# Hymba-style hybrid layer on one core: where the first phase's buffers lie, and where three chunks of W_out are loaded

## The chip, the cores and the metric

One Trainium2 chip (trn2), one of its cores. The metric is the device time of one launch in microseconds; the kernel before took 1374.45 us in the median of 3 runs.

## What is computed

One decoder layer: an input projection, two mixers side by side (windowed attention with sinks, and a Griffin recurrent branch), a gate and a norm for each, an output projection, a residual and a final norm. Everything is float32. Cut to what the change bears on:

```python
h = rmsnorm(x, ln_gain)                                    # x is (1, 2048, 1024)
z = einsum('bsd,de->bse', h, w_in)                         # q | k | v | gate A | recurrent input | gate B
y_attn = swa_sink_attention(q, k, v, sinks)                # window 128, 16 q heads, 4 kv heads of 64
y_attn = rmsnorm(y_attn * silu(g_attn), attn_out_gain)
y_lru = rg_lru(causal_depthwise_conv(x_lru), ...)
y_lru = rmsnorm(y_lru * silu(g_lru), lru_out_gain)
y = einsum('bse,ed->bsd', concatenate([y_attn, y_lru]), w_out)   # 2048 mixed channels to 1024
out = rmsnorm(x + y, final_gain)
```

## The kernel before, in words

Each product in float32 is made of three matmuls: every operand is split into a high part (a copy rounded by ScalarE, type fp32r) and a low part (operand minus high part, made by VectorE, in a few places by GpSimd), and high x high, high x low and low x high are summed in PSUM.

**First phase** (`phase_a`): 16 iterations, four quarters of 512 tokens by four groups of heads and channels. Each iteration projects nine weight groups (24 matmuls of 128x512 each, L1548), runs the attention of four 128-token blocks (`score`, `turn_p`, `weigh_v`), the recurrent gates and the scan, and stores its gated results (`hs0`, `hs1`, `ya`) to a DRAM scratch `y_scratch`, by DMAs that GpSimd issues in `write_out` (L702, L706). The signals `ya_out` and `yl_out` say that these stores have landed. In the last quarter TensorE no longer projects the next group's weights at the end, so the second phase is worked in there.

**Second phase** (`phase_b`): 16 token blocks of 128, two (s = 0, 1) in each of 8 steps. For a block, the 2048 mixed channels are 16 chunks of 128, and a chunk is 6 matmuls of 128x512 (three parts by two halves of the output). Chunks 0 to 7 are the attention's, chunks 8 to 15 the recurrent branch's; their sums stay apart, since each has its own norm, which VectorE multiplies in later (`add_group`).

**W_out** is loaded in 16 chunks of 128x1024 (`OutProjection.load_w`, on SP's DMA queue, L149) into the 3 slots of `w_raw`, chunk e into slot e % 3, each load after `low_w(e - 3)` has freed the slot. ScalarE then makes the high part (`high_w`, L164) and VectorE the low part (`low_w`, L169). Chunks 0 to 7 end in `split` (the first phase's h, free by then), chunks 8 to 15 in `wo_rest`, 64 KB a partition, which lies over the first phase's own buffers.

**The seam.** SP, ScalarE, VectorE, TensorE and GpSimd each run their part of both phases in the order in which it is written, without a barrier. At the start of the second phase ScalarE runs: the squares of block 0's y, `high_w(7)`, the high part of half of block 1's y, then it waits until the first phase is over and its stores have landed, says so (`b.over`), and goes on with `high_w(8)`. VectorE runs `low_w(7)`, `low_w(8)`, and then `mean_y(0, 0)`, the mean square of block 0's y, which it reads from the PSUM bank where TensorE summed it (`sum_squares`, L1998) and which TensorE needs back for chunk 8:

```python
act.wait_ge(*a.ya_done.at(NITER, 0))
act.wait_ge(*a.ya_out.at(NITER, 0))
for u in range(UNITS):
    act.wait_ge(*a.yl_out[u].at(NITER, 0))
act.sem_inc(b.over, 1)
proj.high_w(act, 8)
```

TensorE runs `begin(e)` (chunk e of block 0) and `second(e)` (chunk e of block 1) in the order begin(7), sum_squares(0, 0), begin(8), second(7), begin(9), sum_squares(0, 1), begin(10), begin(11), and then second(8), begin(12), second(9), begin(13), second(10), begin(14), second(11), begin(15), second(12) to second(15). After that comes step(1, 0), which reads `y_own` and waits for `low_y(1, 0)`. SP loads, in this order, chunks 7 to 10, then (after `b.over`) 11, x of block 0 into `res`, chunk 12, y of step 1 (`load_y(1, 0)`), chunks 13 to 15, x of block 1, the final gain (`fgain`), y of block 1 of step 1.

Of the kernel before, what the change touches and what calls it, by code (L numbers as in the profile page):

```python
# [23 lines left out]
F32R = mybir.dt.float32r  # L24
# [6 lines left out]
P = 128  # L31
# [94 lines left out]
ACC = {(0, 0): (0, 1), (1, 0): (2, 3), (0, 1): (0, 1), (1, 1): (2, 3)}  # L126


class OutProjection:


    def __init__(self, nc, both, b, w_out, y_dram):
        self.nc, self.both, self.b, self.w_out, self.y_dram = nc, both, b, w_out, y_dram
        blocks = lambda ap: ap.rearrange("p s d -> p (s d)").rearrange("p (e t) -> p e t", e=EC)
        self.y_raw = [blocks(both.rows[:, :, :]), blocks(both.rope[:, :, :])]
        self.y_hi = [both.y_own[:, 0, :, :], blocks(both.w_hi[:, 0:2, :])]
        self.y_lo = [both.y_own[:, 1, :, :], blocks(both.w_lo[:, 0:2, :])]
        self.first = both.split[:, :, :, :].rearrange("p q w (c d) -> p q w c d", c=4)
        self.rest = None

    def wo(self, e, low):
        if e >= EC // 2:
            return self.rest[:, e - EC // 2, low, :]
        return self.first[:, e // 4, low, e % 4, :]

    def load_w(self, sp, e):
        if e >= WSLOTS:
            sp.wait_ge(*self.b.wo_low.at(e - WSLOTS, 1))
        sp.dma_start(self.both.w_raw[:, e % WSLOTS, :], self.w_out[0, e * P:(e + 1) * P, :]  # L149
                     ).then_inc(*self.b.wo_in[e % WSLOTS].one())  # L150

    def load_y(self, sp, m, s):
# [8 lines left out]
    def high_w(self, act, e):  # L161
        s = e % WSLOTS
        act.wait_ge(*self.b.wo_in[s].at(e // WSLOTS, 1))
        self.nc.scalar.activation(self.wo(e, 0), self.both.w_raw[:, s, :], ACT.Copy,  # L164
                                  scale=self.both.egain[:, e:e + 1]).then_inc(*self.b.wo_high.one())

    def low_w(self, dve, e):
        dve.wait_ge(*self.b.wo_high.at(e, 1))
        self.nc.vector.scalar_tensor_tensor(  # L169
            out=self.wo(e, 1), in0=self.both.w_raw[:, e % WSLOTS, :], scalar=self.both.egain[:, e:e + 1],  # L170
            in1=self.wo(e, 0).bitcast(F32), op0=ALU.mult, op1=ALU.subtract).then_inc(*self.b.wo_low.one())

    def high_y(self, act, m, s):
# [100 lines left out]
def phase_a(nc, top, block, both, signals_b, proj, x, ln_gain, w_tiles, sinks, w_gates,  # L274
# [9 lines left out]
    with ExitStack() as ctx:  # L284
        signals = []

        def sb(name, shape, dt=F32):
            return ctx.enter_context(nc.sbuf_tensor(name, shape, dt))
# [10 lines left out]
        xs = sb("x_stat", [P, 4])
        table_sink = sb("table_sink", [P, 1])  # L300
        cosT, sinT, kraw, swp = (both.rope[:, i, :] for i in range(4))
        prev_mask = sb("prev_mask", [P, GQ, BLK], U8)
        cap = sb("cap", [P, 2, BLK])
        sink_all = sb("sink_all", [P, KV * GQ])
        sink_pairs = sink_all[:, :].rearrange("p (j s) -> p j s", s=2)
        prm = sb("prm", [P, NPRM, LRU_W // P])
# [4 lines left out]
        kc_ol = sb("kc_ol", [P, KV, BLK])
        k_carry, o_low = kc_ol[0:HD], kc_ol[HD:]
        vraw = sb("vraw", [P, 1 + NBLK, HD])
        v_hl = sb("v_hl", [P, 1 + NBLK, 2 * HD], F32R)
        dvraw = sb("dvraw", [P, NBLK, HD])
        dv_hl = sb("dv_hl", [P, NBLK, 2 * HD], F32R)
        v_carry = sb("v_carry", [P, KV, HD])
        qraw = sb("qraw", [P, T])
        qrot = sb("qrot", [P, T])
        q_hi = sb("q_hi", [P, 2, T], F32R)  # L320
        q_lo = sb("q_lo", [P, 2, T], F32R)

        s_sb = sb("s_sb", [P, 2, GQ, BLK + 1])
        p_sb = sb("p_sb", [P, 2, GQ, BLK + 1])
        smax = sb("smax", [P, 2, 4, GQ])
        sden = sb("sden", [P, 2, 2, GQ])
        p_hi = sb("p_hi", [P, GQ, BLK], F32R)
        p_lo = sb("p_lo", [P, GQ, BLK], F32R)
        p_hi_c = sb("p_hi_c", [P, GQ, BLK], F32R)
        p_lo_c = sb("p_lo_c", [P, GQ, BLK], F32R)  # L330
        o_sb = sb("o_sb", [P, 2, BLK])
        ya = sb("ya", [P, 2, T])
        xl = sb("xl", [P, CONV - 1 + T])
        cu = [sb(f"cu{u}", [P, T]) for u in range(UNITS)]
        u_hi = sb("u_hi", [P, T], F32R)
        u_lo = sb("u_lo", [P, T], F32R)
# [3 lines left out]
        ra = [sb(f"ra{u}", [P, T]) for u in range(UNITS)]  # L340
        a2 = sb("a2", [P, T])
        ri_all = sb("ri", [P, UNITS, T])
        ri = [ri_all[:, u, :] for u in range(UNITS)]
        gl = sb("gl", [P, T])
        hs = [sb(f"hs{u}", [P, T]) for u in range(UNITS)]
# [1361 lines left out]
        done.o_sum = o_sum  # L1707
        done.ya_out = ya_out
        done.yl_out = yl_out
        done.zeroed = zeroed  # L1710
        return done


def signals_of_phase_b(nc, top):
    b = Record()
    b.all = []

    def signal(name, per, unit=1):
# [24 lines left out]
    b.mean = signal("mean", 2)
    b.rooted = signal("rooted", 2)
    b.recip = signal("recip", 2)
    b.normed = signal("normed", 2)
    b.res_free = [signal(f"res_free{s}", 1) for s in range(2)]

    b.stored = [Signal(top, nc, f"stored{s}", 1, 16, lead=0) for s in range(2)]
    sem = lambda name: top.enter_context(nc.semaphore(name))  # L1750
    (b.half_product, b.half_added, b.half_sq, b.half_mean, b.half_root, b.half_normed, b.half_out) = (
        sem("half_" + s) for s in ("product", "added", "sq", "mean", "root", "normed", "out"))
    b.over, b.fgain_in, b.settled = sem("phase_a_over"), sem("fgain_in"), sem("settled_b")
    return b


def phase_b(nc, block, both, b, proj, a, x, final_gain, out):

    ones = both.ones
    with ExitStack() as ctx:  # L1760
        def sb(name, shape, dt=F32):
            return ctx.enter_context(nc.sbuf_tensor(name, shape, dt))

        proj.rest = sb("wo_rest", [P, EC // 2, 2, D], F32R)
        res = sb("res", [P, 2, D])
        fgain = sb("fgain", [P, D])
# [17 lines left out]
        def _(sp):  # L1784
# [48 lines left out]
        def _(act):  # L1833
# [58 lines left out]
        def _(dve):  # L1892
# [233 lines left out]
```

## Time and profile before

| | |
|---|---|
| median of 3 runs | 1374.45 us (1372.53 to 1374.49) |
| profiled execution, its own time | 1375.38 us |
| its span, first to last instruction | 1373.7 us |
| granted TensorE clock, mean | 0.998 |
| TensorE busy with matmuls | 1353.7 us (99%) |
| VectorE, ScalarE, GpSimd busy | 970.2, 845.6, 217.2 us |
| DMA | 243.22 MB, mean 177 GB/s |

The profiled execution's time is 1.7 us more than its span, and 0.9 us above the median. PE is TensorE's matmuls and PEld its weight loads, DVE is VectorE, ACT ScalarE, POOL GpSimd; SPq is the queue on which SyncE issues DMAs. In a row of the timeline, a "[4.3 <-X]" is time for which the engine sat idle and what ended it.

### The profile page before, as it was taken

How to read it: one execution, taken by the hardware profiler on the slowest of the kernel's cores; microseconds unless marked ns; L12 is line 12 of the kernel's file. 1: busy time of each engine (PE TensorE's matmuls, PEld its weight loads, DVE VectorE, ACT ScalarE, POOL GpSimd, SP SyncE). 2: the span in 40 equal slices, each digit the busy share in tenths (PEclk: the TensorE clock that was granted, in tenths of full speed). 3: DMA queues.
4: the chain of work that ended last, by engine and by line, in shares of the span. 5: the costliest groups of instructions: out<-in, count | busy, mean ns of one | idle time of the engine just before them, and what ended most of it. 6: DMA issues, size and time to landing. Idle time of an engine off the chain costs nothing.

```text
span 1373.7 us, 22283 instructions
## 1 busy us (share of the span) xinstructions
PE 1353.7 (99%) x6756; PEld 1107.4 (81%) x6756; DVE 970.2 (71%) x1668; ACT 845.6 (62%) x1729; POOL 217.2 (16%) x247
## 2 busy tenths in 40 slices
PE   8999999999999999999999999999989999999998
PEld 7777877888888888888888878888867888888886
DVE  5998999968686877868687767878686544434442
ACT  7888797867777685867777585766764221222120
POOL 2020212112130312113031212213020000000000
PEclk9999999999999999999999999999999999999999
DMA  8766768655554555454555655354535423324120
GB/s 323 260 226 246 274 225 288 230 188 173 183 178 177 203 184 200 158 187 172 184 186 184 224 202 211 135 206 164 193 114 193 138 86 97 98 86 121 62 92 31
DMA packets 98289, 243.22 MB, mean 177 GB/s; under 512 B 8112, under 2 KB 43056, under 8 KB 98224
## 3 DMA queue, kind: packets, MB, share of 16 engines
q1 hardware_dynamic: 91200, 217.79, 46.9%
q0 software_dynamic: 7024, 24.65, 4.5%
q8 instruction: 31, 0.51, 0.2%
q14 instruction: 34, 0.28, 0.1%
HBM read 179.49 MB, written 62.91 MB: 176 GB/s over the span
## 4 chain that ended last, share of the span: by engine, by line
PE 85%; DVE 3%; ACT 2%; issue 1%; DMA 1%; DVEq 0%; ACTq 0%; POOL 0%; POOLq 0%
PE ring L1548 50%; PE acc_b L223 12%; PE ring L223 11%; PE ps_tv L1611 4%; PE ps_s L1587 3%; PE ps_tv L1598 2%; PE ring L1625 2%; PE ps_tv L1587 1%; PE ring L1635 1%; DMA y_scratch<-ya 1%; PE ring L1560 0%; DMA w_raw<-w_out_d 0%; DVE o_sb L1318 0%; PE acc_b L1998 0%; DVE cu L1340 0%
## 5 line engine op out<-in xcount | busy, mean ns | idle before, releaser
L1548 PE MATMUL ring<-split,w_hi 128*128 128x512 f32 x2288 | 717.1, 395 | 1.1 <-DVE w_lo L1082 0.4
L1548 PEld LDWEIGHTS ring<-split,w_hi 128*128 128x128 f32 x2288 | 421.3, 188 | 97.5 <-issue 8.9
L1548 PE MATMUL ring<-split,w_lo 128*128 128x512 f32 x1144 | 446.6, 390 | 0.0
L1548 PEld LDWEIGHTS ring<-split,w_lo 128*128 128x128 f32 x1144 | 214.7, 188 | 45.9
L663 POOL TENSOR_SCALAR_AFFINE_SELECT p_hi_c<-p_hi 128x512 fp32r<-128x512 f32 x64 | 41.5, 648 | 518.1 <-ACT p_hi L891 518.1
L883 ACT ACTIVATE p_sb<-s_sb,smax 128x129 f32<-128x129 f32 x256 | 99.6, 392 | 0.6
L1840 ACT ACTIVATE w_hi<-res 128x1024 fp32r<-128x1024 f32 x15 | 15.9, 1060 | 132.3 <-DVE res L1913 132.3
L223 PE MATMUL acc_b<-wo_rest,y_own 128*128 128x512 f32 x384 | 90.8, 393 | 5.4 <-DVE rms L1898 4.3
L223 PE MATMUL ring<-split,y_own 128*128 128x512 f32 x384 | 91.5, 392 | 0.0
L1340 DVE SCALAR_TENSOR_TENSOR cu<-xl,prm,cu 128x512 f32<-128x512 f32 x96 | 72.2, 752 | 26.6 <-ACT cu L910 20.0
L223 PEld LDWEIGHTS acc_b<-wo_rest,y_own 128*128 128x128 f32 x384 | 72.2, 189 | 21.3 <-DVE rms L1898 4.4
L223 PEld LDWEIGHTS ring<-split,y_own 128*128 128x128 f32 x384 | 71.4, 188 | 14.7
L1913 DVE SCALAR_TENSOR_TENSOR res<-acc_b,rms,res 128x1024 f32<-128x1024 f32 x15 | 19.3, 1284 | 79.5 <-PE acc_b L223 79.5
L223 PE MATMUL ring<-split,w_hi 128*128 128x512 f32 x256 | 70.3, 397 | 0.0
L223 PE MATMUL acc_b<-wo_rest,w_hi 128*128 128x512 f32 x256 | 69.7, 389 | 0.0
L663 POOL TENSOR_SCALAR_AFFINE_SELECT p_lo_c<-p_lo 128x512 fp32r<-128x512 f32 x64 | 60.2, 941 | 46.8 <-DVE p_lo L1309 45.6
L896 ACT ACTIVATE kc_ol<-ps_tv 64x512 f32<-64x512 f32 x64 | 38.0, 593 | 35.4 <-PE ps_tv L1611 33.3
L1823 POOL DMA_DIRECT2D out_d<-res x15 | 8.0, 536 | 323.6 <-DVE res L1923 323.6
L1318 DVE TENSOR_TENSOR o_sb<-ps_tv,kc_ol 64x256 f32<-64x256 f32 x128 | 53.4, 417 | 5.2
L1280 DVE COPY_PREDICATED s_sb<-prev_mask,ps_s 128x512 f32<-128x512 uint8 x48 | 35.6, 742 | 29.4 <-ACT s_sb L875 28.8
L223 PEld LDWEIGHTS acc_b<-wo_rest,w_hi 128*128 128x128 f32 x256 | 48.0, 188 | 10.0
L223 PEld LDWEIGHTS ring<-split,w_hi 128*128 128x128 f32 x256 | 48.0, 190 | 9.9 <-issue 0.2
(249 smaller groups left out, 2420.5 us busy)
## 6 DMA issues: line engine op xcount, KB each, us to landing
w_hi<-w_split_scratch SPq DMA_DIRECT2D x108, 512.0 KB, 3.3
w_lo<-w_split_scratch SPq DMA_DIRECT2D x108, 512.0 KB, 4.3
w_raw<-w_tiles_d SPq DMA_DIRECT2D x36, 512.0 KB, 4.3
w_split_scratch<-w_hi SPq DMA_DIRECT2D x36, 512.0 KB, 5.0
w_split_scratch<-w_lo SPq DMA_DIRECT2D x36, 512.0 KB, 5.7
y_scratch<-hs POOLq DMA_DIRECT2D x32, 256.0 KB, 6.2
y_scratch<-ya POOLq DMA_DIRECT2D x16, 512.0 KB, 6.0
rows<-y_scratch SPq DMA_DIRECT2D x8, 1024.0 KB, 7.8
```

The source lines that it names most:

```text
L223: last = self.nc.tensor.matmul(banks[:, ACC[s, g][h], :], y[s][:, e, :], self.wo(e, low)[:, h * (D // 2):(h + 1) * (D // 2)], start=(e % ( ...
L663: nc.gpsimd.affine_select(out=dst[:, :, :], in_=f(src[:, :, :]), compare_op=ALU.is_ge, fill=0.0, base=0, pattern=[[0, GQ], [1, BLK]], chan ...
L883: nc.scalar.activation(p_sb[:, b % 2, h, :], s_sb[:, b % 2, h, :], ACT.Exp, bias=smax[:, b % 2, 0, h:h + 1], accum_out=sden[:, b % 2, 0, h ...
L896: nc.scalar.activation(o_low, ps_v[HD:, :, :], ACT.Copy).then_inc(*o_lowdone.one())
L1280: nc.vector.copy_predicated(s, prev_mask[:, :, :], scores_of(b)[:, :, 0:BLK]).then_inc(*s_sel.one())
L1318: nc.vector.tensor_tensor(o_sb[s * HD:(s + 1) * HD, :, :], pair(ps_v[0:HD], s), pair(o_low, s), ALU.add).then_inc(*o_sum.one())
L1340: stt(out=cu[u][:, :], in0=xl[:, tap:tap + T], scalar=prm[:, C_W0 + tap, bass.ds(G, 1)], in1=cu[u][:, :], op0=ALU.mult, op1=ALU.add).then_ ...
L1548: last = mm(bank(r), w[:, i % WSLOTS, k, :], h[:, par, k, :], start=(k == 0 and j == 0), stop=(k == KC - 1 and j == 2))
L1587: last = mm(scores_of(b)[:, 2 * half + j, :], v[rows, j, b * BLK:(b + 1) * BLK], k[rows, b * BLK:(b + 2) * BLK], start=(i == 0), stop=(i = ...
L1598: last = nc.tensor.transpose(ps_t[:, h, :], p_sb[:, b % 2, h, 0:BLK], ident[:, :])
L1611: last = mm(ps_v[:, :, :], v[:, b, :], p[:, :, :], start=(i == 0), stop=(i == 3))
L1625: ins = mm(bank((R_R, R_I)[half][u]), w[rows, u, :], v[rows, :], start=(i == 0), stop=(i == 2))
```

## The change

The first phase's SBUF buffers are allocated in another order: q, k and the raw q first, then the recurrent branch's, the attention's, and last the buffers that are stored to DRAM. The second phase's small statistics, `res` and `fgain` are allocated before `wo_rest`, and so lie over `q_hi`, `q_lo`, `krot` and part of `k_hi`. Chunks 7, 8 and 9 of W_out are loaded into `res[0]`, `res[1]` and `fgain` rather than into `w_raw`; chunks 10 and later keep their slot e % 3. `b.over` is gone: each load, conversion and store of the second phase waits for the first phase's signal on the buffers that it overwrites, and the loads that later fill `res` and `fgain` wait until the chunk that lay there is split.

```diff
+ASIDE = (7, 8, 9)
...
+    def raw(self, e):
+        return self.aside[e] if e in ASIDE else self.both.w_raw[:, e % WSLOTS, :]
     def load_w(self, sp, e):
         if e >= WSLOTS:
-            sp.wait_ge(*self.b.wo_low.at(e - WSLOTS, 1))
-        sp.dma_start(self.both.w_raw[:, e % WSLOTS, :], self.w_out[0, e * P:(e + 1) * P, :]
+            sp.wait_ge(*self.b.wo_in[e % WSLOTS].at(e // WSLOTS - 1, 1))
+            if e not in ASIDE:
+                front = e - WSLOTS if e - WSLOTS not in ASIDE else e - 2 * WSLOTS
+                sp.wait_ge(*self.b.wo_low.at(front, 1))
+        sp.dma_start(self.raw(e), self.w_out[0, e * P:(e + 1) * P, :]
...
-        proj.rest = sb("wo_rest", [P, EC // 2, 2, D], F32R)
+        rms = sb("rms", [P, 2, 3, 2])
+        stat = sb("stat", [P, 2, 4])
         res = sb("res", [P, 2, D])
         fgain = sb("fgain", [P, D])
-        rms = sb("rms", [P, 2, 3, 2])
-        stat = sb("stat", [P, 2, 4])
+        proj.rest = sb("wo_rest", [P, EC // 2, 2, D], F32R)
+        proj.aside.update(zip(ASIDE, (res[:, 0, :], res[:, 1, :], fgain[:, :])))
...
-            for e in range(7, 10):
+            sp.wait_ge(*a.scores.at(NITER, 0))
+            for e in ASIDE:
                 proj.load_w(sp, e)
-            proj.load_w(sp, 10)
-            sp.wait_ge(b.over, 1)
-            proj.load_w(sp, 11)
+            for e in range(10, 13):
+                proj.load_w(sp, e)
+            sp.wait_ge(*b.wo_low.at(7, 1))
             load_x(0, 0)
-            proj.load_w(sp, 12)
+            proj.load_w(sp, 13)
+            sp.wait_ge(*a.ya_out.at(NITER, 0))
+            for u in range(UNITS):
+                sp.wait_ge(*a.yl_out[u].at(NITER, 0))
             proj.load_y(sp, 1, 0)
-            for e in range(13, EC):
+            for e in range(14, EC):
                 proj.load_w(sp, e)
+            sp.wait_ge(*b.wo_low.at(8, 1))
             load_x(0, 1)
+            sp.wait_ge(*b.wo_low.at(9, 1))
...
-            act.wait_ge(*a.ya_done.at(NITER, 0))
-            act.wait_ge(*a.ya_out.at(NITER, 0))
-            for u in range(UNITS):
-                act.wait_ge(*a.yl_out[u].at(NITER, 0))
-            act.sem_inc(b.over, 1)
+            act.wait_ge(*a.scores.at(NITER, 0))
             proj.high_w(act, 8)
             proj.square_y(act, 0, 1, 0)
+            act.wait_ge(*a.one_minus.at(NITER, 0))
+            act.wait_ge(*a.ring_ready.at(NITER - 1, R_I1 + 1))
             proj.high_w(act, 9)
             proj.square_y(act, 0, 1, 1)
+            act.wait_ge(*a.i_x.at(NITER, 0))
             proj.high_w(act, 10)
+            act.wait_ge(*a.scanned.at(NITER, 0))
+            act.wait_ge(*a.yl_done.at(NITER, 0))
             proj.high_w(act, 11)
             root_y(0, 0)
-            for e in range(12, EC):
+            proj.high_w(act, 12)
+            act.wait_ge(*a.pv.at(NITER, 0))
+            act.wait_ge(*a.ya_done.at(NITER, 0))
+            for e in range(13, EC):
                 proj.high_w(act, e)
...
-            for e in range(13, EC):
+            for e in range(13, EC - 1):
                 proj.low_w(dve, e)
+            for u in range(UNITS):
+                dve.wait_ge(*a.yl_out[u].at(NITER, 0))
+            proj.low_w(dve, EC - 1)
```

SP's queue at the start of the second phase, before (`w_raw<-w_out_d` is a chunk of W_out, `rows<-y_scratch` is y of step 1, and x4 are chunks 7 to 10):

```order
L149 DMA w_raw<-w_out_d 128x1024 [waits wo_low] x4
L149 DMA w_raw<-w_out_d 128x1024 [waits wo_low,phase_a_over]
L1787 DMA res<-x_d 128x1024 [waits res_free0]
L149 DMA w_raw<-w_out_d 128x1024 [waits wo_low]
L158 DMA rows<-y_scratch 128x16x128 [waits y_low,y_sq]
L149 DMA w_raw<-w_out_d 128x1024 [waits wo_low] x3
```

and with the change:

```order
L162 DMA res<-w_out_d 128x1024 [waits wo_in1,scores]
L162 DMA res<-w_out_d 128x1024 [waits wo_in2]
L162 DMA fgain<-w_out_d 128x1024 [waits wo_in0]
L162 DMA w_raw<-w_out_d 128x1024 [waits wo_low,wo_in1]
L162 DMA w_raw<-w_out_d 128x1024 [waits wo_low,wo_in2]
L162 DMA w_raw<-w_out_d 128x1024 [waits wo_low,wo_in0]
L1806 DMA res<-x_d 128x1024 [waits res_free0,wo_low]
L162 DMA w_raw<-w_out_d 128x1024 [waits wo_low,wo_in1]
L171 DMA rows<-y_scratch 128x16x128 [waits y_low,yl_out1,ya_out,yl_out0,y_sq]
L162 DMA w_raw<-w_out_d 128x1024 [waits wo_low,wo_in2]
L162 DMA w_raw<-w_out_d 128x1024 [waits wo_low,wo_in0]
```

The loads of chunks 7 to 9 no longer wait for a split chunk, chunks 10 to 12 wait for the low parts of 4 to 6, chunk 13 now stands ahead of y of step 1, and the wait for the first phase's stores has moved from chunk 11 to y.

ScalarE at the same place, before (the first row is `high_w(7)`, and the rows on `wo_rest` are `high_w(8)` and on):

```order
L164 ACTIVATE split<-w_raw,egain 128x1024 [waits wo_in1]
L202 ACTIVATE sqy<-rows 128x1024 [waits y_in0,y_part]
L188 ACTIVATE w_hi<-rope 128x1024 [waits product1,y_in1,ring_ready]
L164 ACTIVATE wo_rest<-w_raw,egain 128x1024 [waits yl_out1,yl_out0,ya_done,ya_out,wo_in2]
L202 ACTIVATE sqy<-rope 128x1024 [waits y_in1,y_part]
L164 ACTIVATE wo_rest<-w_raw,egain 128x1024 [waits wo_in0]
```

and with the change:

```order
L177 ACTIVATE split<-res,egain 128x1024 [waits wo_in1]
L215 ACTIVATE sqy<-rows 128x1024 [waits y_in0,y_part]
L201 ACTIVATE w_hi<-rope 128x1024 [waits product1,y_in1,ring_ready]
L177 ACTIVATE wo_rest<-res,egain 128x1024 [waits wo_in2,scores]
L215 ACTIVATE sqy<-rope 128x1024 [waits y_in1,y_part]
L177 ACTIVATE wo_rest<-fgain,egain 128x1024 [waits wo_in0,ring_ready,one_minus]
```

The instructions and their order are the same; `high_w(8)` waits for the last scores instead of the landed stores. The orders of TensorE and GpSimd are unchanged, waits included, and VectorE's only gets the wait for `yl_out` ahead of `low_w(15)`.

## Rows read from the trace of the kernel before

**Rows 1.** The page, part 1: busy time of each engine

```profile
PE 1353.7 (99%) x6756; PEld 1107.4 (81%) x6756; DVE 970.2 (71%) x1668; ACT 845.6 (62%) x1729; POOL 217.2 (16%) x247
```

**Rows 2.** Waits of TensorE, whole run: us in total, times, longest

```profile
PE acc_b L223 <- DVE rms L1898: 4.3, 1, 4.3
...
PE acc_b L223 <- DVE wo_rest L169: 1.1, 1, 1.1
```

**Rows 3.** Windows: length, busy of PE, PEld, DVE, ACT, POOL, granted clock, DMA share, GB/s

```profile
1024.30:1028.50 4.20, 0.00 (x0) 0.00 (x0) 1.40 (x4) 2.58 (x3) 0.00 (x0) 1.00 0.16 64
1028.50:1031.00 2.50, 2.43 (x7) 1.89 (x8) 2.43 (x6) 0.55 (x1) 0.00 (x0) 0.60 0.59 203
...
1033.00:1035.00 2.00, 2.00 (x12) 1.65 (x10) 1.86 (x4) 1.98 (x3) 0.00 (x0) 1.00 0.72 253
...
1042.00:1043.40 1.40, 0.28 (x2) 0.08 (x1) 1.40 (x2) 1.15 (x1) 0.00 (x0) 1.00 1.03 401
```

**Rows 4.** Timeline of TensorE at the seam: start, length (us), then the instruction

```profile
1023.77 0.50 PE L1998 MATMUL acc_b<-ones,part 128*128 128x1 f32 x4
1028.57 2.56 PE L223 MATMUL acc_b<-wo_rest,y_own 128*128 128x512 f32 x6 [4.31 <-DVE rms L1898]
1030.94 1.78 PE L223 MATMUL ring<-split,w_hi 128*128 128x512 f32 x4
...
1043.32 1.66 PE L223 MATMUL acc_b<-wo_rest,y_own 128*128 128x512 f32 x6 [1.12 <-DVE wo_rest L169]
...
1046.17 1.52 PE L223 MATMUL acc_b<-wo_rest,y_own 128*128 128x512 f32 x6
1047.53 1.07 PE L223 MATMUL acc_b<-wo_rest,w_hi 128*128 128x512 f32 x4
...
1055.69 2.66 PE L223 MATMUL ring<-split,y_own 128*128 128x512 f32 x11
```

**Rows 5.** Timeline of ScalarE at the seam

```profile
1020.85 1.04 ACT L188 ACTIVATE w_hi<-rope 128x1024 fp32r<-128x1024 f32 x1
1025.92 1.15 ACT L164 ACTIVATE wo_rest<-w_raw,egain 128x1024 fp32r<-128x1024 f32 x1 [4.03 <-POOLq L712]
...
1040.79 2.41 ACT L164 ACTIVATE wo_rest<-w_raw,egain 128x1024 fp32r<-128x1024 f32 x2 [3.68 <-DMA w_raw<-w_out_d]
```

**Rows 6.** Timeline of VectorE at the seam

```profile
1027.10 1.28 DVE L169 SCALAR_TENSOR_TENSOR wo_rest<-w_raw,egain,wo_rest 128x1024 fp32r<-128x1024 f32 x1 [4.64 <-ACT wo_rest L164]
1028.30 0.22 DVE L1898 TENSOR_SCALAR rms<-acc_b 128x1 f32<-128x1 f32 x2
...
1030.95 1.28 DVE L169 SCALAR_TENSOR_TENSOR wo_rest<-w_raw,egain,wo_rest 128x1024 fp32r<-128x1024 f32 x1
...
1033.56 1.28 DVE L169 SCALAR_TENSOR_TENSOR wo_rest<-w_raw,egain,wo_rest 128x1024 fp32r<-128x1024 f32 x1
...
1052.55 2.29 DVE L180 TENSOR_TENSOR y_own<-rows,y_own 128x2048 fp32r<-128x2048 f32 x1 [0.72 <-ACT y_own L176]
```

**Rows 7.** Timeline of GpSimd: the first phase's last store to DRAM

```profile
1018.59 0.71 POOL L706 DMA_DIRECT2D y_scratch<-ya  x1 [0.19 <-issue]
```

**Rows 8.** Timeline of SP's queue: DMA issues around the seam

```profile
999.07 0.33 SPq L149 DMA_DIRECT2D w_raw<-w_out_d  x1
...
1018.49 0.33 SPq L149 DMA_DIRECT2D w_raw<-w_out_d  x1
...
1032.26 0.33 SPq L149 DMA_DIRECT2D w_raw<-w_out_d  x1
1032.78 0.38 SPq L158 DMA_DIRECT2D rows<-y_scratch  x1
1034.87 1.85 SPq L149 DMA_DIRECT2D w_raw<-w_out_d  x2
```

**Rows 9.** The tile w_raw from 985 to 1050 us: DMA issue to landing

```profile
DMA to landing us min/median/max: 3.1/5.2/6.2
```

**Rows 10.** A window of 100 us in the first quarter: columns as in group 3

```profile
100.00:200.00 100.00, 98.28 (x520) 79.35 (x519) 91.05 (x149) 84.22 (x171) 14.77 (x16) 1.00 0.70 250
```

More of the change, by code:

```diff
@@ L137, in __init__ @@
         self.y_lo = [both.y_own[:, 1, :, :], blocks(both.w_lo[:, 0:2, :])]
+        self.aside = {}
         self.first = both.split[:, :, :, :].rearrange("p q w (c d) -> p q w c d", c=4)
@@ L163, in high_w @@
         act.wait_ge(*self.b.wo_in[s].at(e // WSLOTS, 1))
-        self.nc.scalar.activation(self.wo(e, 0), self.both.w_raw[:, s, :], ACT.Copy,
+        self.nc.scalar.activation(self.wo(e, 0), self.raw(e), ACT.Copy,
                                   scale=self.both.egain[:, e:e + 1]).then_inc(*self.b.wo_high.one())
@@ L169, in low_w @@
         self.nc.vector.scalar_tensor_tensor(
-            out=self.wo(e, 1), in0=self.both.w_raw[:, e % WSLOTS, :], scalar=self.both.egain[:, e:e + 1],
+            out=self.wo(e, 1), in0=self.raw(e), scalar=self.both.egain[:, e:e + 1],
             in1=self.wo(e, 0).bitcast(F32), op0=ALU.mult, op1=ALU.subtract).then_inc(*self.b.wo_low.one())
@@ L296, in signal @@
             return s
[L299 to L306, printed above, removed]
+        q_hi = sb("q_hi", [P, 2, T], F32R)
+        q_lo = sb("q_lo", [P, 2, T], F32R)
         krot = sb("krot", [HD, BLK + T])
@@ L309, in phase_a @@
         k_lo = sb("k_lo", [P, BLK + T], F32R)
[L311 to L317, printed above, removed]
         qraw = sb("qraw", [P, T])
         qrot = sb("qrot", [P, T])
-        q_hi = sb("q_hi", [P, 2, T], F32R)
-        q_lo = sb("q_lo", [P, 2, T], F32R)
+        xl = sb("xl", [P, CONV - 1 + T])
+        a2 = sb("a2", [P, T])
+        gw_raw = sb("gw_raw", [P, UNITS, P])
+        gw_hi = sb("gw_hi", [P, UNITS, P], F32R)
+        gw_lo = sb("gw_lo", [P, UNITS, P], F32R)
+        u_hi = sb("u_hi", [P, T], F32R)
+        u_lo = sb("u_lo", [P, T], F32R)
+        vraw = sb("vraw", [P, 1 + NBLK, HD])
+        dvraw = sb("dvraw", [P, NBLK, HD])
+        v_carry = sb("v_carry", [P, KV, HD])
+        cu = [sb(f"cu{u}", [P, T]) for u in range(UNITS)]
+        ra = [sb(f"ra{u}", [P, T]) for u in range(UNITS)]
+        ri_all = sb("ri", [P, UNITS, T])
+        ri = [ri_all[:, u, :] for u in range(UNITS)]
+        gl = sb("gl", [P, T])
+        v_hl = sb("v_hl", [P, 1 + NBLK, 2 * HD], F32R)
+        dv_hl = sb("dv_hl", [P, NBLK, 2 * HD], F32R)
         s_sb = sb("s_sb", [P, 2, GQ, BLK + 1])
         p_sb = sb("p_sb", [P, 2, GQ, BLK + 1])
-        smax = sb("smax", [P, 2, 4, GQ])
-        sden = sb("sden", [P, 2, 2, GQ])
         p_hi = sb("p_hi", [P, GQ, BLK], F32R)
@@ L330, in phase_a @@
         p_lo_c = sb("p_lo_c", [P, GQ, BLK], F32R)
[L331 to L336, printed above, removed]
         by_token = lambda w: w[:, :, :].rearrange("p h t -> p (h t)")
         u_parts = [(u_hi[:, :], u_lo[:, :]), (by_token(p_hi), by_token(p_lo))]
[L340 to L345, printed above, removed]
+        kc_ol = sb("kc_ol", [P, KV, BLK])
+        k_carry, o_low = kc_ol[0:HD], kc_ol[HD:]
+        prev_mask = sb("prev_mask", [P, GQ, BLK], U8)
+        cap = sb("cap", [P, 2, BLK])
+        smax = sb("smax", [P, 2, 4, GQ])
+        sden = sb("sden", [P, 2, 2, GQ])
         x_carry = sb("x_carry", [P, LRU_W // P, CONV - 1])
         h_carry = sb("h_carry", [P, LRU_W // P, 1])
-        gw_raw = sb("gw_raw", [P, UNITS, P])
-        gw_hi = sb("gw_hi", [P, UNITS, P], F32R)
-        gw_lo = sb("gw_lo", [P, UNITS, P], F32R)
+        xs = sb("x_stat", [P, 4])
+        table_sink = sb("table_sink", [P, 1])
+        sink_all = sb("sink_all", [P, KV * GQ])
+        sink_pairs = sink_all[:, :].rearrange("p (j s) -> p j s", s=2)
+        o_sb = sb("o_sb", [P, 2, BLK])
+        prm = sb("prm", [P, NPRM, LRU_W // P])
+        hs = [sb(f"hs{u}", [P, T]) for u in range(UNITS)]
+        ya = sb("ya", [P, 2, T])
+        cosT, sinT, kraw, swp = (both.rope[:, i, :] for i in range(4))
         ring = both.ring
@@ L1709, in phase_a @@
         done.yl_out = yl_out
-        done.zeroed = zeroed
+        done.scores, done.pv, done.one_minus, done.i_x = scores, pv, one_minus, i_x
+        done.scanned, done.yl_done = scanned, yl_done
         return done
@@ L1752, in signals_of_phase_b @@
         sem("half_" + s) for s in ("product", "added", "sq", "mean", "root", "normed", "out"))
-    b.over, b.fgain_in, b.settled = sem("phase_a_over"), sem("fgain_in"), sem("settled_b")
+    b.fgain_in, b.settled = sem("fgain_in"), sem("settled_b")
     return b
```

## The prediction

> **What bounds the kernel.** I read the page first, for the bound. TensorE is busy for 1353.7 of 1373.7 us [rows 1], so only what shortens TensorE's idle or slow time can shorten the kernel. The view of waits, TensorE's alone, says where 20 us of idle time can be got back: its longest wait of the whole run is 4.3 us, once, for VectorE's `mean_y` (L1898), and another is 1.1 us, once, for a low part of W_out [rows 2]. Both lie at the seam of the phases. The windows there show the first as an empty stretch, and show what follows it: the granted clock is 0.60 from 1028.5 to 1031.0 us, so part of it at the lower of its two levels (1.2 GHz instead of 2.4 GHz), and 1.00 again by 1033. After the 1.1 us gap the clock stayed at 1.00 [rows 3].
>
> The timelines give the chain, read backwards. TensorE ends its sums of squares at 1024.26 and starts chunk 8 at 1028.57 [rows 4]. It waits for `mean_y`, which ran at 1028.30, right behind `low_w(8)` at 1027.10, which waited for `high_w(8)` [rows 6]. That started at 1025.92 after 4.03 us of idling, ended by GpSimd's word that the stores have landed; ScalarE's instruction before it had started at 1020.85 and taken 1.04 us [rows 5]. The last store was issued only at 1018.59 [rows 7]. So a DMA of y to DRAM holds up a conversion of W_out, and that only because `wo_rest` lies over buffers which those stores read.
>
> **How much there is to get.** From 1024.26 to 1055.69, where step(1, 0) begins, TensorE runs 17 chunks and one pair of sums. A chunk at the full clock takes 1.36 us (1046.17 to 1047.53), the sums 0.49 us (1023.77 to 1024.26) [rows 4]: 23.1 + 0.5 = 23.6 us in 31.43. The excess, 7.8 us, is 4.3 of the first wait, 1.7 of chunk 8 and second(7) at the lower clock (1028.57 to 1030.94 is 2.37 us, and the next ends at 1033.02, 2.08 us, instead of 1.36 each), 0.3 of ramp, and some 1.4 around the second wait.
>
> **The change, part by part.**
>
> *`high_w(8)` without the stores.* Its new conditions are the scores, done before 1000 us, and the chunk's own data. Chunks 7 to 9 are now issued behind chunk 6, which goes out at 999.07 [rows 8]; at 3.1 to 6.2 us each [rows 9] all three are in by about 1010. ScalarE starts `high_w(8)` when the y half ends, near 1021.85, and VectorE can start `low_w(8)` at about 1023.0 instead of 1027.10. From there VectorE's order is unchanged and ran back to back, so I shift it rigidly by 4.1 us: `low_w(9)` ended at 1030.95 + 1.28 = 1032.23 and now ends at 1028.15; `low_w(10)` ended at 1034.84 and now at 1030.75 [rows 6]; `low_w(11)`, one more of 1.28 behind a short mean, at 1032.3.
>
> *`high_w(7)`* starts 0.7 us earlier because its data is there. Cost and gain nothing: ScalarE's next instruction waits for VectorE's sum of squares, which is not moved.
>
> *TensorE with this.* `mean_y` needs the sums (1024.26) and the end of `low_w(8)` (1024.28); from its start to TensorE's start was 0.27 us, so chunk 8 starts at 1024.57: 0.3 us idle. Two chunks end at 1027.29. Chunk 9 must now wait for `low_w(9)`, 1028.2: 0.9 us idle, and 0.13 of slower restart, as after the second wait. It ends at 1029.7, the sums at 1030.2. Chunk 10 waits for `low_w(10)` until 1030.8, 0.6 us, and chunk 11 for 0.1; it ends at 1033.7. So the one long wait becomes four short ones, and VectorE sets them. Five more chunks follow, to 1040.5. Chunks 12 and 13 are there by then: 12 is issued when the low part of 6 is done, at 1018.49, where SP issued chunk 9 before [rows 8], and 13 as soon as `low_w(10)` is done, at 1031.0 instead of 1034.87.
>
> *Chunk 14.* It is what is late next. It is issued at 1032.4, behind chunk 13 and the 1 MB of y. Before, the same three transfers (half, whole and half a MB) stood in the queue as chunk 12 at 1032.26, y at 1032.78 and chunk 13 at 1034.87 [rows 8], and the last of them landed at about 1040.77, when ScalarE started on it [rows 5]: 8.5 us after the first. From there to TensorE's start at 1043.32 [rows 4] is 2.55 us. Now the first is issued at 1031.0, so chunk 14 lands at 1039.5 and TensorE can use it at 1042.05, 1.55 us after it is ready for it, and restarts 0.13 slower. It ends at 1043.55, and the last six chunks at 1051.7. Chunk 15 comes right behind 14 and isn't late. The gain is 1055.69 − 1051.7 = **4.0 us**.
>
> The bounds of this term: at the least time from issue to landing, 3.1 us [rows 9], chunk 14 isn't waited for and the gain is 5.6 us; if it lands 2 us later than I have it, as a transfer that found y's stream still running might, the gain is 2.0. I take the row of the same three transfers.
>
> The Trainium skill (DMA: Bandwidth & Descriptors, Anatomy of one DMA) fits a transfer as 2.0 us plus its bytes at 436 GB/s, measured on GpSimd's queue. By that fit the three would be in 6.8 us after the first issue, at 1037.8, and there would be no wait: the sum would be 5.6 us. Its section on queues says that descriptors of one queue are consumed in ring order; by that rule the trace agrees, the chunk behind y being the one that came late.
>
> *The other moved waits.* y of step 1 now stands behind chunk 13, so behind `low_w(10)`, and is issued near 1031.5 instead of 1032.78; its wait for the stores (done at 1025.9) is over by then. x of block 0 goes out after `low_w(7)`, at 1021.1, and is needed at about 1034. x of block 1, the final gain and y of block 1 go out 3 to 5 us earlier than before. Nothing queued on SP behind these is needed sooner. VectorE's new wait before `low_w(15)` is over 18 us early. Nothing of it is on the path.
>
> *After the seam.* step(1, 0) waits for `low_y(1, 0)`, which starts only when chunk 15 of block 0 is done. It ended at 1052.55 + 2.29 = 1054.84 [rows 6], 0.85 us before TensorE was there; chain and cover both hang on chunk 15, so they move together. Behind it TensorE has no wait of that size [rows 2], so the gain reaches the end.
>
> *The new addresses.* Every buffer of the first phase moves. The same instructions run on the same shapes and partitions; I cost it at nothing.
>
> **The sum.** The profiled execution had a span of 1373.7 and a time of 1375.38; the change would make them 1369.7 and 1371.4. The median was 0.93 us below that execution, so I predict 1370.4.
>
> **The rivals.**
>
> *Chunk 14 isn't late* (13%). For it: the DMA stream at the seam starts from idle and earlier. Against it: so it did before. It gives 5.6 us, 1368.9.
>
> *The clock falls all the same* (9%). Four gaps sum to 1.9 us within 7. For it: one gap of 4.3 us brought the clock down. Against it: 1.1 us did not [rows 3], and the four are apart. The price is that of before, 1.7 us, less what the waits for VectorE absorb: a gain of 2.3, 1372.1. The Trainium skill (TensorE: Matmul & The Clock Gate, Part 1) has the lower clock as the default that activity lifts, which leaves this open.
>
> *It doesn't do what it says* (10%). Another condition holds the seam, such as data of chunk 8 or 9 that comes late, or a wait of step 1 that takes the gain back. Against it: the loads have 12 us to spare and the margin of 0.85 us moves along. The gain would be 0 to 2 us, about 1373.5.
>
> *Slower through the addresses* (4%). If VectorE ran slower on buffers at their new places, the first quarter would show it, where VectorE is busy for 91 of 100 us and TensorE for only 98.3 [rows 10]. That load lasts some 200 us, so each 1% there adds up to 1.8 us; it cancels the gain at 2.2% and makes the kernel measurably slower at 3.8%. At 5% the time is 1379.5. Nothing in the trace speaks for it.
>
> **How the numbers follow.** A change of under 0.2%, 2.7 us, can't be told from none. The forecast has 64%: 1370.4, and nearly always over the bound, 58 of the 64. Faster: 58 + 13 + 3 of the clock's + 1 = 75%. Same: 6 + 6 + 9 = 21%. Slower: 4%. The range runs from the gain of 5.6 with 0.7 for the scatter of runs, 1368.2, to a gain of 2.0 with the rest of the scatter, 1373.0.
>
> **What would show it.** Right: no wait of TensorE for `mean_y` over 0.5 us; waits of about 1 us before chunk 9 and under 1 before chunk 10, on `wo_rest`; the granted clock at 1.00 through the seam; one wait of 1 to 2 us before chunk 14, ended by a DMA on ScalarE's side; step(1, 0) some 4 us earlier, and the same first phase to within 0.3 us. Wrong: a clock of 0.5 or 0.6 after 1028, a wait at step(1, 0), or a first phase that is longer by microseconds.

## The result: 0.28% slower, where 0.3% faster was forecast

| | before | changed |
|---|---|---|
| median of 7 runs each | 1374.49 us (1372.53 to 1375.51) | 1378.63 us (1375.32 to 1379.98) |
| ratio | | 1.0028, 95% interval 1.0016 to 1.0040 |
| span of the profiled execution | 1373.7 us | 1378.4 us |
| TensorE busy with matmuls | 1353.7 us | 1361.3 us |

The change lost 4.1 us; the forecast was a gain of 4.0. TensorE's row on the page of the changed kernel answers to [rows 1]:

```profile
PE 1361.3 (99%) x6756; PEld 1108.2 (80%) x6756; DVE 969.7 (70%) x1668; ACT 845.0 (61%) x1729; POOL 217.4 (16%) x247
```

The same 6756 matmuls are busy for 7.6 us longer. More waiting can't do that; slower matmuls can. (Not all of the 7.6 is slower matmuls: in the first 100 us of this execution TensorE idled less and was busy for 96.0 us instead of 94.3.) TensorE's waits in the changed kernel, between 1015 and 1070 us (total, times, longest), answer to [rows 2]:

```profile
PE acc_b L236 <- DVE wo_rest L182: 4.4, 3, 3.2
PE acc_b L236 <- DVE rms L1933: 0.3, 1, 0.3
```

The wait of 4.3 us for `mean_y` is down to 0.3, as forecast, but the waits for low parts of W_out have grown from 1.1 to 4.4 us, 3.2 of them in one. The timeline of TensorE shows where, as [rows 4] did:

```profile
1023.27 0.50 PE L2037 MATMUL acc_b<-ones,part 128*128 128x1 f32 x4
1024.09 1.67 PE L236 MATMUL acc_b<-wo_rest,y_own 128*128 128x512 f32 x6 [0.32 <-DVE rms L1933]
...
1027.80 1.67 PE L236 MATMUL acc_b<-wo_rest,y_own 128*128 128x512 f32 x6 [0.66 <-DVE wo_rest L182]
...
1030.41 3.06 PE L236 MATMUL acc_b<-wo_rest,y_own 128*128 128x512 f32 x12 [0.59 <-DVE wo_rest L182]
...
1043.64 2.23 PE L236 MATMUL acc_b<-wo_rest,y_own 128*128 128x512 f32 x6 [3.17 <-DVE wo_rest L182]
1045.67 1.91 PE L236 MATMUL acc_b<-wo_rest,w_hi 128*128 128x512 f32 x4
...
1055.10 1.09 PE L236 MATMUL ring<-split,y_own 128*128 128x512 f32 x4
```

The forecast waits before chunks 8, 9, 10 and 14 are there (that of 0.1 us before chunk 11 doesn't show). The seam, from the first sums of squares to step(1, 0), took 1055.69 − 1023.77 = 31.9 us before and 1055.10 − 1023.27 = 31.8 us now: all that chunk 8 won was lost again at chunk 14 and behind it, where the clock fell too. (This is one execution, the slowest of the seven.) The windows (columns as in [rows 3]) show that:

```profile
1040.30:1043.60 3.30, 0.17 (x1) 0.00 (x0) 1.28 (x1) 2.34 (x3) 0.00 (x0) 1.00 0.98 353
1043.60:1046.00 2.40, 2.36 (x7) 1.95 (x8) 1.36 (x2) 0.05 (x1) 0.00 (x0) 0.69 0.97 276
1046.00:1048.00 2.00, 2.00 (x6) 1.54 (x6) 0.00 (x0) 0.00 (x0) 0.00 (x0) 0.52 0.94 237
1048.00:1050.00 2.00, 2.00 (x11) 1.59 (x10) 0.21 (x1) 0.23 (x1) 0.00 (x0) 1.00 0.02 5
```

That explains why nothing was won, not what was lost. **The loss lies behind the seam**: from step(1, 0) to the end it is 1373.7 − 1055.7 = 318.0 us before and 1378.4 − 1055.1 = 323.3 us now, though TensorE waits for nothing from there to its last matmul in either. Before and changed, the same window of the second phase:

```profile
1100.00:1200.00 100.00, 100.00 (x452) 82.95 (x450) 43.31 (x68) 26.35 (x34) 2.66 (x5) 1.00 0.30 91
```

```profile
1100.00:1200.00 100.00, 100.00 (x445) 81.69 (x444) 41.64 (x67) 26.05 (x34) 2.66 (x5) 1.00 0.29 89
```

TensorE is full and at the full clock in both, and does 445 matmuls instead of 452. The timelines say which are slow. (A matmul has a stationary operand, which PEld loads, here a 128x128 piece of `y_own`, `w_hi` or `w_lo`, and a moving operand of 512 columns, here from `split` or `wo_rest`.) Block 0 of one step, before (24 matmuls of chunks 0 to 3, 24 of 4 to 7, 48 of 8 to 15):

```profile
1100.23 5.60 PE L223 MATMUL ring<-split,y_own 128*128 128x512 f32 x24
1106.03 5.75 PE L223 MATMUL ring<-split,y_own 128*128 128x512 f32 x24
1111.61 11.04 PE L223 MATMUL acc_b<-wo_rest,y_own 128*128 128x512 f32 x48
```

and changed:

```profile
1100.38 5.64 PE L236 MATMUL ring<-split,y_own 128*128 128x512 f32 x24
1106.21 5.75 PE L236 MATMUL ring<-split,y_own 128*128 128x512 f32 x24
1111.80 11.38 PE L236 MATMUL acc_b<-wo_rest,y_own 128*128 128x512 f32 x48
```

It is the 48 whose moving operand is `wo_rest` that are slower, by 0.34 us; start to start they take some 233 ns instead of 227. Fourteen blocks behind the seam make 4.8 us of the 5.3; the rest is in the first 24 matmuls of the blocks, on `split`, 0.04 us a block. The operand, the shapes, the order and the clock are the same. What is new is its address: `wo_rest` began at byte 142048 of each partition, right behind `y_own`, and begins now at 154432, 12384 further up (the order and sizes of the buffers in kernel.py give the difference). All other operands of these matmuls (`split`, `w_hi`, `w_lo`, `y_own`) are where they were.

### The profile page after: what moved, and what is told of

Same layout as the page of the kernel before. It is cut to its first block, busy times and chain, and to the rows that moved or that the text cites. A ratio compares the mean times of both kernels' runs of the same rounds, so it can differ in the third digit from the quotient of the medians.

```text
span 1378.4 us, 22300 instructions
## 1 busy us (share of the span) xinstructions
PE 1361.3 (99%) x6756; PEld 1108.2 (80%) x6756; DVE 969.7 (70%) x1668; ACT 845.0 (61%) x1729; POOL 217.4 (16%) x247
## 4 chain that ended last, share of the span: by engine, by line
PE 83%; DVE 2%; ACT 1%; DMA 1%; issue 1%; POOL 0%; DVEq 0%; ACTq 0%; POOLq 0%; SPq 0%
PE ring L1565 48%; PE acc_b L236 12%; PE ring L236 12%; PE ps_tv L1628 4%; PE ps_s L1604 2%; PE ps_tv L1615 2%; PE ring L1642 2%; DMA w_raw<-w_out_d 1%; PE ring L1652 1%; PE ps_tv L1604 1%; PE ring L1577 0%; PE acc_b L2037 0%; DVE wo_rest L182 0%; DVE cu L1357 0%; DVE o_sb L1335 0%
## 5 line engine op out<-in xcount | busy, mean ns | idle before, releaser
L1357 DVE SCALAR_TENSOR_TENSOR cu<-xl,prm,cu 128x512 f32<-128x512 f32 x96 | 72.2, 752 | 26.8 <-ACT cu L927 20.2
L1297 DVE COPY_PREDICATED s_sb<-prev_mask,ps_s 128x512 f32<-128x512 uint8 x48 | 35.6, 742 | 29.4 <-ACT s_sb L892 29.0
L236 PEld LDWEIGHTS ring<-split,w_hi 128*128 128x128 f32 x256 | 47.4, 188 | 10.1
```

The source lines that it names most:

```text
L236: last = self.nc.tensor.matmul(banks[:, ACC[s, g][h], :], y[s][:, e, :], self.wo(e, low)[:, h * (D // 2):(h + 1) * (D // 2)], start=(e % ( ...
L1297: nc.vector.copy_predicated(s, prev_mask[:, :, :], scores_of(b)[:, :, 0:BLK]).then_inc(*s_sel.one())
L1357: stt(out=cu[u][:, :], in0=xl[:, tap:tap + T], scalar=prm[:, C_W0 + tap, bass.ds(G, 1)], in1=cu[u][:, :], op0=ALU.mult, op1=ALU.add).then_ ...
```

## The experiments

In all of them "rest" is the time from step(1, 0) to the end and "seam" the time from the first sums of squares to step(1, 0), both from the profiled execution; ratios are to the kernel before on the same chip.

### Does the address make the matmuls slow, and which part of it?

The first theory was about the start address alone: 142048 is 32 past a multiple of 64, 154432 is a multiple of 64. Its rivals: what counts is the distance between stationary and moving operand, or the region. The edit is an unused buffer, of 32 or 64 bytes:

```diff
+        pad = sb("pad", [P, 8])
         proj.rest = sb("wo_rest", [P, EC // 2, 2, D], F32R)
```

and for b_all32 the same ahead of `w_raw`, so that all operands of the second phase's products move by 32 bytes. In the kernel before, `res`, `fgain` and the small statistics lie behind `wo_rest` and move with it.

> The changed kernel with an unused buffer of 32 bytes a partition ahead of wo_rest, which then starts at 154464 instead of 154432. Start theory (a moving operand that starts at a multiple of 64 bytes streams slower than one that starts 32 past it): the matmuls on wo_rest go back from 233 to 227 ns start to start, from step(1, 0) to the end it takes 318 us instead of 323, and the kernel about 1373.5, the seam as in the changed kernel. Region theory (wo_rest is slow because it lies some 12 KB further up, whatever its low address bits): still 233 ns and about 1378.6.

> The kernel before with an unused buffer of 32 bytes ahead of wo_rest, which then starts at 142080 (a multiple of 64) instead of 142048. Start theory: the matmuls on wo_rest take 233 ns instead of 227, 48 of them in each of 16 token blocks, so about 5 us more: 1379.5. Relative theory (what counts is that stationary and moving operand start at the same place modulo 64): the same here. Region theory: 1374.5, no change.

> The kernel before with an unused buffer of 32 bytes ahead of w_raw, so that w_hi, w_lo, split, y_own and wo_rest all move from 32 past a multiple of 64 to a multiple of 64. Start theory: all matmuls with a moving operand of 512 columns take some 6 ns more, about 5,000 of them: 1374.5 + 25 to 30 us. Relative theory: stationary and moving operand still start alike, no change, 1374.5. Region theory: no change.

> The kernel before with 64 unused bytes ahead of wo_rest, which starts at 142112, again 32 past a multiple of 64. Start and relative theory with a period of 64 bytes: 227 ns and 1374.5, no change. If the period is 128 bytes or more: between 1374.5 and 1380. Region theory: no change.

| | `wo_rest` moved by | rest | median | ratio and interval |
|---|---|---|---|---|
| a_pad32 | 12416 | 322.6 us | 1377.21 us | 1.0020 (1.0010 to 1.0029) |
| b_pad32 | 32 | 323.0 us | 1380.66 us | 1.0038 (1.0026 to 1.0051) |
| b_all32 | 32, with all others | 318.0 us | 1373.99 us | 0.9998 (0.9989 to 1.0008) |
| b_pad64 | 64 | 320.5 us | 1377.28 us | 1.0021 (1.0011 to 1.0030) |

b_pad32 is the plainest: 32 bytes that nobody uses make the kernel before slower by 6.4 us (its own chip's median before is 1374.23) and its rest 5.0 us longer, nearly the 5.3 of the change with all its moves. b_all32 has `wo_rest` at the very same address and loses nothing, so the first theory falls, and so does the region. The distance between the operands is left. Blocks of b_pad32 and b_all32:

```profile
1112.73 11.37 PE L223 MATMUL acc_b<-wo_rest,y_own 128*128 128x512 f32 x48
```

```profile
1110.62 11.04 PE L223 MATMUL acc_b<-wo_rest,y_own 128*128 128x512 f32 x48
```

### Over what period?

> The kernel before with wo_rest 128 bytes further up. Start theory is out: with every operand moved by 32 bytes the pace stayed at 227 ns, and 64 bytes between the operands cost time. Relative theory: the matmul's stationary operand (512 bytes a partition) and its moving operand (2048 bytes) are slow together unless they start at the same place modulo some period. Period 128: 227 ns on wo_rest and 318 us from step(1, 0) to the end. Longer period: 229 to 234 ns and 320 to 324 us.

> As the last, 256 bytes. Period 128 or 256: 227 ns, 318 us from step(1, 0) to the end. Period 512 or more: 229 to 234 ns and 320 to 324 us.

> As the last, 512 bytes. Period 512 or a divisor: 227 ns, 318 us from step(1, 0) to the end. If it is slow too, the period is over 512 bytes (1, 2 or 4 KB), or what counts is not a period but that wo_rest no longer follows y_own directly.

> The changed kernel with 416 unused bytes ahead of wo_rest, so that it lies 12800 bytes, 25 times 512, further up than in the kernel before. Period 512 or a divisor: 227 ns on wo_rest, 318 us from step(1, 0) to the end and about 5.3 us less than the changed kernel: 1373.5 us. Longer period: still slow, about 1377 to 1379.

| | `wo_rest` moved by | modulo 256 | rest |
|---|---|---|---|
| b_pad128 | 128 | 128 | 322.6 us |
| b_pad256 | 256 | 0 | 318.0 us |
| b_pad512 | 512 | 0 | 318.0 us |
| a_pad416 | 12800 | 0 | 318.1 us |

With the four above and the changed kernel itself: at distances of 32, 64, 96 and 128 bytes modulo 256 the rest is 320.5 to 323.3 us, at 0 it is 318.0 or 318.1. So 128 bytes isn't the period and 256 fits; 160, 192 and 224 weren't tried. a_pad416 shows that this is the whole loss behind the seam: the changed kernel with 416 unused bytes takes 1372.39 us, 0.9985 of before (0.9975 to 0.9994). b_pad128, b_pad256 and b_pad512 had one run each and are read by their traces.

### Each matmul's own pair?

In all of these `wo_rest` moved against every stationary operand. b_yown32 has the unused 32 bytes ahead of `y_own`, so that `y_own` and `wo_rest` move together, and `split`, `w_hi` and `w_lo` stay. Block 0 has `y_own` as stationary operand, block 1 `w_hi` and `w_lo`.

> The kernel before with 32 unused bytes ahead of y_own, so that y_own and wo_rest lie 32 bytes further up, and split, w_hi and w_lo where they were. Pair theory (a matmul is slow when its own stationary and moving operand don't start alike modulo 256 bytes): block 0 of each step (stationary y_own) takes 227 ns on wo_rest and 230 to 234 on split, block 1 (stationary w_hi and w_lo) 230 to 234 ns on wo_rest and 227 on split. Rival (wo_rest is slow wherever it is not at its old place modulo 256, whatever the stationary operand): 230 to 234 ns on wo_rest in both blocks, 227 on split in both.

Block 0 of b_yown32:

```profile
1102.70 5.76 PE L223 MATMUL ring<-split,y_own 128*128 128x512 f32 x24
1108.65 5.83 PE L223 MATMUL ring<-split,y_own 128*128 128x512 f32 x24
1114.33 11.05 PE L223 MATMUL acc_b<-wo_rest,y_own 128*128 128x512 f32 x48
```

and two chunks of each kind of its block 1:

```profile
1133.91 1.07 PE L223 MATMUL ring<-split,w_hi 128*128 128x512 f32 x4
1135.27 1.07 PE L223 MATMUL ring<-split,w_hi 128*128 128x512 f32 x4
...
1138.03 1.09 PE L223 MATMUL acc_b<-wo_rest,w_hi 128*128 128x512 f32 x4
1139.43 1.10 PE L223 MATMUL acc_b<-wo_rest,w_hi 128*128 128x512 f32 x4
```

In block 0 the pair `y_own` and `wo_rest` is fast again (11.05 us) and `y_own` with `split` is slow (5.76 instead of 5.60); in block 1 it is the other way round, 1.36 us a chunk on `split` and 1.40 on `wo_rest`. All four outcomes are the pair theory's. The rival wanted `wo_rest` slow in both blocks. The one run of b_yown32 took 1381.41 us.

Inside a block, though, a matmul's own stationary operand and the one that is loaded while it runs, the next matmul's, come from the same buffer, so these outcomes don't say which of the two counts. The end of block 0 does, in part. Its last matmul has `y_own` and `wo_rest`, which are aligned in b_yown32, and the next has `w_hi`, which lies 32 bytes off `wo_rest`. The last matmul of block 0 and its successor in b_yown32, and the same two in the kernel before:

```profile
1124.98 0.40 PE L223 MATMUL acc_b<-wo_rest,y_own 128*128 128x512 f32 x1
1125.22 0.39 PE L223 MATMUL ring<-split,w_hi 128*128 128x512 f32 x1
```

```profile
1122.27 0.39 PE L223 MATMUL acc_b<-wo_rest,y_own 128*128 128x512 f32 x1
1122.49 0.39 PE L223 MATMUL ring<-split,w_hi 128*128 128x512 f32 x1
```

In all seven steps of b_yown32 whose block 0 lies behind the seam this matmul takes 235 ns start to start, against 226 or 227 before: its own pair is aligned, and it is slow. So the pair that counts is not the own one alone; the load of the next stationary operand, which PEld makes beside the running matmul, bears on it. It isn't that load alone either as far as this trace goes: at the six changes from block 1 to the next block 0, where the own pair is 32 bytes off and the next is aligned, it takes 233 or 234 ns.

### Why the seam won so little

Chunk 14 was forecast to land at 1039.5. ScalarE's timeline, and SP's queue, of the changed kernel:

```profile
1034.13 1.15 ACT L177 ACTIVATE wo_rest<-w_raw,egain 128x1024 fp32r<-128x1024 f32 x1 [1.85 <-DMA w_raw<-w_out_d]
1041.12 2.44 ACT L177 ACTIVATE wo_rest<-w_raw,egain 128x1024 fp32r<-128x1024 f32 x2 [5.83 <-DMA w_raw<-w_out_d]
```

```profile
1030.42 0.33 SPq L162 DMA_DIRECT2D w_raw<-w_out_d  x1
1031.02 0.38 SPq L171 DMA_DIRECT2D rows<-y_scratch  x1
1031.75 6.30 SPq L162 DMA_DIRECT2D w_raw<-w_out_d  x2
1038.14 0.38 SPq L1806 DMA_DIRECT2D res<-x_d  x1
```

From the first issue to the landing it is 1041.12 − 1030.42 = 10.7 us, where the same three transfers (half a MB, y's 1 MB, half a MB) had taken 8.5 before. The issue of chunks 14 and 15, right behind y, took SP 6.3 us instead of 0.33 each. The long issue isn't what makes chunk 14 late: in a_pad416 the two took 2.6 us together and the landing still 10.1. An estimate from the Trainium skill's fit (DMA: Bandwidth & Descriptors, Anatomy of one DMA), 2.0 us and the three transfers' bytes at 436 GB/s, is 6.8 us; here the trace doesn't agree. The remedy is to put y behind the chunks:

```diff
-            proj.load_w(sp, 13)
+            for e in range(13, EC):
+                proj.load_w(sp, e)
...
             proj.load_y(sp, 1, 0)
-            for e in range(14, EC):
-                proj.load_w(sp, e)
```

It was run with the pad (c_wfirst), without it (a_wfirst), and on the kernel before (b_wfirst). c_dve adds two moves to c_wfirst: ScalarE's `high_w(8)` ahead of `high_y_group(0, 1, 1)`, and VectorE's `low_y_group(0, 1, 1)` behind `low_w(11)` instead of ahead of the sums.

> The last kernel (changed, 416 bytes ahead of wo_rest) with chunks 13, 14 and 15 issued ahead of y of step 1. Queue theory (chunk 14 is late because the 1 MB of y, in pieces of 512 bytes, stands ahead of it and holds up its issue): chunk 14 lands within 4 us of its issue near 1031, the wait of 2.8 us before it is gone, y still comes 5 us before it is needed: seam (first sums to step(1, 0)) 26.5 us instead of 29.4, kernel 1369.5. Rival (chunk 14 is late through the DMAs' total rate): it lands at most 1 us earlier and the kernel stays within 1 us of 1372.4.

> The one before, and in addition ScalarE makes the high part of chunk 8 ahead of that of y's half, and VectorE makes y's low half behind the low part of chunk 11 instead of ahead of chunk 9's. Theory (VectorE's order from chunk 8 on sets TensorE's remaining short waits): the chain starts 0.5 us earlier, and the 1.2 us of y's half lie beside chunk 11: seam 1 to 1.7 us shorter than in the one before, kernel about 1368. Rival (the low part that second(8) needs is then what comes last): no change against the one before.

> The kernel before with chunks 13 to 15 issued ahead of y of step 1, nothing else. Queue theory: chunk 13 no longer has y ahead of it, the wait of 1.1 us before it goes: seam 31.9 to about 30.5 us, kernel 1373. Rival: no change, 1374.5.

> The changed kernel, its own addresses, with chunks 13 to 15 ahead of y. If addresses and seam add up: 5.2 us of slower matmuls on wo_rest from step(1, 0) on remain, the seam is 27 us, so about 5 us less than the changed kernel: 1373.7, no different from the kernel before.

| | seam | rest | median | ratio and interval |
|---|---|---|---|---|
| changed | 31.8 us | 323.3 us | 1378.63 us | 1.0028 (1.0016 to 1.0040) |
| a_pad416 | 29.4 | 318.1 | 1372.39 | 0.9985 (0.9975 to 0.9994) |
| a_wfirst | 26.8 | 323.3 | 1375.16 | 1.0010 (1.0000 to 1.0019) |
| c_wfirst | 26.6 | 318.0 | 1369.66 | 0.9963 (0.9949 to 0.9977) |
| c_dve | 25.2 | 318.1 | 1368.68 | 0.9953 (0.9936 to 0.9969) |
| b_wfirst | 31.4 | 318.0 | 1374.14 | 0.9995 (0.9985 to 1.0004) |

TensorE's waits in c_wfirst, and in c_dve, from 1015 to 1070 us:

```profile
PE acc_b L236 <- DVE wo_rest L182: 1.3, 2, 0.7
PE acc_b L236 <- DVE rms L1933: 0.3, 1, 0.3
```

```profile
PE acc_b L236 <- DVE wo_rest L182: 0.5, 1, 0.5
PE acc_b L236 <- DVE rms L1932: 0.3, 1, 0.3
```

The wait before chunk 14 is gone, and 2.8 us of seam with it: chunk 14, issued at 1031.93, landed at 1036.3, 3.6 us earlier than in a_pad416, where the rival of the DMAs' total rate allowed 1. So it was y ahead of it in the queue that made it late; whether through its size or through its small pieces isn't shown, since y was only moved as a whole. The two parts add up in the traces: a_wfirst has the short seam with the slow rest, a_pad416 the fast rest with the longer seam, c_wfirst both gains. In the median a_wfirst is 1.5 us above the 1373.7 expected. The two moves of c_dve, ScalarE's and VectorE's 1.2 us beside chunk 11, took another 1.4 us of seam, within the 1 to 1.7 expected; they ran together and aren't told apart. b_wfirst lost the wait before chunk 13 but not 1.4 us of seam, only 0.5: its first wait was 4.5 us instead of 4.3, with a slow clock behind it as before, and in the median it can't be told from the kernel before. Nor can the lost wait be put down to the queue: b_all32 and b_pad256, whose queue is that of the kernel before, had no wait there either (seams of 31.9 and 32.1 us).

**c_dve is the best version that ran**, 1368.68 us: 5.8 us under the kernel before and 10 under the change as made.

## Why the prediction was wrong, step by step

*What bounds the kernel:* right. TensorE is the bound, and its wait for `mean_y` could be had.

*`high_w(8)` without the stores:* right. It started at 1021.30 without a wait, and `low_w(8)` at 1022.47; with the changed kernel's first phase 0.5 us earlier (scatter: the same sums start between 1021.4 and 1025.3 us in kernels that share that phase), that is the 1023.0 forecast. The waits before chunks 8, 9 and 10 were forecast at 0.3, 0.9 and 0.6 us and measured 0.32, 0.66 and 0.59.

*Chunk 14:* right in kind, too small in size, and a step that failed too. The term was 1.55 us plus 0.13 and measured 3.17, with some 1.6 of slower clock behind it. I took the landing from one earlier occurrence, 8.5 us, gave it 2 us of bound to the late side and let it cost no clock; it took 10.7 us. In a_pad416, with the right addresses, the same transfer took 10.1 and the wait was 2.79 us, so that the seam gained 2.5 us instead of 4.0.

*"The new addresses. [...] I cost it at nothing":* the step that failed and turned the gain into a loss. It cost 5.3 us behind the seam and, at 0.04 us for each of 16 chunks, some 0.6 of the seam's gain; the rest of the 2.4 us between the seams of the changed kernel and a_pad416 is the later chunk 14 and the clock, which differ between executions (a_pad32, with slow addresses too, had a seam of 30.9 us). The reason given (the same instructions on the same shapes and partitions) is no reason, as b_pad32 shows with 32 unused bytes. The rival "slower through the addresses" had the right side and the wrong engine: it looked for the loss in VectorE and the first quarter, and found nothing in the trace for it. The trace of the kernel before couldn't have shown the cost: by the sizes of its buffers, `w_hi`, `w_lo`, `split`, `y_own` and `wo_rest` all lay a multiple of 256 bytes apart, and the change broke that for `wo_rest`. Keeping that distance, as a_pad416 does, would have kept the term at nothing.

*The clock's rival:* in part. It fell, not through the short waits but behind the one of 3.17 us. "The granted clock at 1.00 through the seam", a sign of being right, didn't hold.

*The range* doesn't hold the 1378.63: it knew nothing of a cost per matmul. Without that cost (a_pad416) the change gives 1372.39 us, inside the range, 2.3 us under the kernel before on the same chip: the seam's mechanism was right, and gave 2.5 us of the 4.0.

## What to carry to other kernels

When a buffer that feeds matmuls moves, compare TensorE's start-to-start time for that operand before and after; a loss of 3% there hides behind a "busy" engine, and no view of waits shows it. For products like these (float32r, 128x512, a weight load for each) keep stationary and moving operands a multiple of 256 bytes apart, by small unused buffers or by putting small odd-sized buffers last; for others, try it. And on a DMA queue whose next transfer is waited for, put a large one that isn't needed yet behind it, not ahead.

## What the runs showed of the hardware that wasn't expected

- A float32r matmul of 128x512, with its weight load, took 226.7 ns start to start when its stationary and moving operand lay a multiple of 256 bytes apart in the partition, 229 ns at 64 bytes modulo 256 and 233 ns at 32, 96 and 128. It is the distance within the pair at work that counts (b_yown32), not the address (b_all32). Why is open. An aligned matmul took 235 ns where the next stationary operand lay 32 bytes off its moving one, so the load beside it has a part; but one that was 32 bytes off took 233 or 234 where the next was aligned, and other distances, types and shapes weren't tried.
- The length of a gap alone didn't say whether the granted clock falls. A gap of 2.79 us left it at 1.00 (a_pad416), one of 3.17 us was followed by windows at 0.69 and 0.52 (changed kernel), one of 4.31 us by 0.60 [rows 3]; but a shorter one, of 2.34 us at the same place in a_pad32, was followed by 0.83 and 0.50:

```profile
1040.50:1043.00 2.50, 0.19 (x1) 0.00 (x0) 1.28 (x1) 2.36 (x3) 0.00 (x0) 1.00 1.05 381
1043.00:1045.00 2.00, 1.97 (x7) 1.66 (x8) 1.36 (x2) 0.03 (x1) 0.00 (x0) 0.83 1.21 294
1045.00:1047.00 2.00, 2.00 (x6) 1.54 (x6) 0.00 (x0) 0.00 (x0) 0.00 (x0) 0.50 0.48 114
```

- The issue of the DMA right behind y's 1 MB, in pieces of 512 bytes, held SP for 1.0 us (kernel before), 2.1 (a_pad416), 4.6 (changed kernel) and 5.3 (c_wfirst, where x of block 1 stands there), instead of 0.33 to 0.43.
